# A two-block transformer and state-space kernel: the state-space stage as three interleaved chains, and probabilities transposed through a diagonal tile

## What is computed

```python
# MLA, by query block of 128; DSA has the same softmax over its selected keys
s = jnp.where(key_pos[None, :] <= q_pos[:, None], s, -jnp.inf)
p = jax.nn.softmax(s, axis=-1).astype(v.dtype)
return jnp.einsum('bhqk,bkhv->bqhv', p, v)

# ssd_scan, chunks of 128 tokens, 4 groups of 8 heads of 64 channels, state 128
a_cum = jnp.cumsum(adt, axis=2)
seg = a_cum[:, :, :, None] - a_cum[:, :, None, :]
decay = jnp.exp(jnp.where(tri, seg, -jnp.inf))
cb = jnp.einsum("bclgn,bcsgn->bclsg", cm, bm)
y_diag = jnp.einsum("bclsgr,bcsgrp->bclgrp", cb[..., None] * decay, x)
states = jnp.einsum("bclgn,bclgrp->bcgrpn", bm, x * decay_states[..., None])
...                       # recurrence over the 4 chunks gives prev
y_off = jnp.einsum("bclgn,bcgrpn->bclgrp", cm, prev) * jnp.exp(a_cum)[..., None]
y = y_diag + y_off + d_skip * xh
# gated_group_rmsnorm
u = y * jax.nn.silu(z)
u = u * lax.rsqrt(jnp.mean(u * u over the group) + EPS)
y_ssm = (u * g) @ w_ssm_out
merged = jax.nn.sigmoid(g_att) * y_att + jax.nn.sigmoid(g_ssm) * y_ssm
```

## Time and profile before

| | |
|---|---|
| runs, median (lowest to highest), 3 runs | 2856.41 us (2852.3 to 2861.36) |
| the profiled execution | 2849.98 us |
| its span, first to last instruction | 2848.2 us |
| mean granted TensorE clock | 0.962 |
| PE busy | 2662.3 us, 93%, 11724 instructions |
| PEld busy | 2070.7 us, 73% |
| DVE, ACT, POOL busy | 1448.1 (51%), 663.1 (23%), 1142.3 us (40%) |
| DMA | 436.62 MB, 153 GB/s |

### The profile page before, as it was taken

The page is one execution under the profiler, slowest core; times in us unless marked ns, Lnnn a source line. Parts: engine busy times, 40 slices in busy tenths (PEclk is TensorE's granted clock), DMA queues, the critical chain, the costliest instruction groups (busy, mean ns, idle before and its releaser), DMA issues.

```text
span 2848.2 us, 30951 instructions
## 1 busy us (share of the span) xinstructions
PE 2662.3 (93%) x11724; PEld 2070.7 (73%) x11724; DVE 1448.1 (51%) x1985; ACT 663.1 (23%) x1297; POOL 1142.3 (40%) x764
## 2 busy tenths in 40 slices
PE   8999899999999999999999999999888778899998
PEld 6888688888666578888876777766555546688886
DVE  4754574565544435546566744544334447555521
ACT  2004420111233312102132133322213232222200
POOL 4333355555312145555544533322222113455554
PEclk9999999999899999999999999999888879999999
DMA  6433465656312156565644744434433214465565
GB/s 200 125 115 123 129 192 194 193 194 195 122 60 76 43 167 190 194 195 189 210 156 152 229 148 154 157 126 133 159 123 117 96 45 140 146 195 194 191 195 168
DMA packets 148857, 436.62 MB, mean 153 GB/s; under 512 B 13872, under 2 KB 18160, under 8 KB 148720
## 3 DMA queue, kind: packets, MB, share of 16 engines
q1 hardware_dynamic: 64224, 200.29, 23.9%
q0 software_dynamic: 67584, 201.35, 20.2%
q10 hardware_dynamic: 16912, 33.14, 3.2%
HBM read 417.90 MB, written 16.83 MB: 153 GB/s over the span
## 4 chain that ended last, share of the span: by engine, by line
issue 38%; PE 32%; POOL 23%; DVE 3%; DMA 2%; ACT 2%; DVEq 1%; ACTq 0%; POOLq 0%; SPq 0%
POOL w_lo L450 18%; PE bank L502 9%; PE bank L504 8%; PE bank L505 8%; POOL w_hi L432 5%; PE bank L703 1%; DMA projections<-spill_out 1%; PE bank L1117 1%; PE bank L777 0%; PE bank L780 0%; PE bank L779 0%; DMA residual<-x_in 0%; PE bank L1077 0%; DVE next_gained L2234 0%; PE bank L1107 0%
## 5 line engine op out<-in xcount | busy, mean ns | idle before, releaser
L450 POOL TENSOR_TENSOR w_lo<-w_raw,w_hi 128x1024 fp32r<-128x1024 f32 x376 | 908.9, 2418 | 15.1 <-DMA w_hi<-stream 7.1
L432 POOL DMA_DIRECT2D w_hi<-stream x376 | 227.2, 604 | 1673.1 <-PE bank L502 1505.4
L502 PE MATMUL bank<-x_hi,w_hi 128*128 128x512 f32 x1472 | 590.5, 401 | 26.8 <-POOL w_lo L450 13.5
L504 PE MATMUL bank<-x_lo,w_hi 128*128 128x512 f32 x1472 | 578.6, 393 | 0.0
L505 PE MATMUL bank<-x_hi,w_lo 128*128 128x512 f32 x1472 | 578.0, 393 | 0.0
L502 PEld LDWEIGHTS bank<-x_hi,w_hi 128*128 128x128 f32 x1472 | 279.8, 190 | 96.9 <-issue 20.9
L505 PEld LDWEIGHTS bank<-x_hi,w_lo 128*128 128x128 f32 x1472 | 279.6, 190 | 59.7
L504 PEld LDWEIGHTS bank<-x_lo,w_hi 128*128 128x128 f32 x1472 | 279.9, 190 | 57.5 <-issue 2.4
L1983 DVE TENSOR_TENSOR relu_sq<-relu 128x512 f32<-128x512 f32 x64 | 179.1, 2799 | 94.6 <-ACT relu L1395 94.6
L502 PE MATMUL bank<-hidden_hi,w_hi 128*128 128x512 f32 x512 | 199.2, 389 | 0.0
L504 PE MATMUL bank<-hidden_lo,w_hi 128*128 128x512 f32 x512 | 199.2, 389 | 0.0
(11 more groups left out here) (435 smaller groups left out, 4450.8 us busy)
## 6 DMA issues: line engine op xcount, KB each, us to landing
w_hi<-stream POOLq DMA_DIRECT2D x376, 512.0 KB, 4.8
w_raw<-stream SPq DMA_DIRECT2D x376, 512.0 KB, 3.7
projections<-spill_out ACTq DMA_DIRECT2D x56, 256.0 KB, 2.0
ssm_x<-projections ACTq DMA_DIRECT2D x4, 1024.0 KB, 7.2
gate_tiles<-projections ACTq DMA_DIRECT2D x16, 256.0 KB, 3.2
ssm_z<-projections ACTq DMA_DIRECT2D x4, 1024.0 KB, 9.5
residual<-x_in SPq DMA_DIRECT2D x4, 512.0 KB, 10.7
toeplitz_hi<-toeplitz_rows_hi POOLq DMA_DIRECT2D x4, 512.0 KB, 6.5
```

The costliest lines, as they stand in the source:

```text
L432: e.dma_start(in_slot(whi, t % SLOTS, o), in_stream(o)).then_inc(hi_ready[t % SLOTS], 16)
L450: e.tensor_tensor(wlo[:, s, :], raw[:, s, :], whi[:, s, :].bitcast(F32), ALU.subtract).then_inc(lo_ready, 1)
L502: mm = e.matmul(out, wh, rh, start=first, stop=False)
L504: e.matmul(out, wh, rl, start=False, stop=False)
```

## The change

**Transposes.** In both attentions VectorE no longer scales the row of exponentials. It multiplies the 128x128 identity by the column of inverse sums, and TensorE multiplies each 128x128 tile of exponentials by this diagonal tile, which transposes and scales at once. The call is `matmul` with float32 operands where it was `transpose`.

**State space.** The phases become one sequence of 16 head-pair steps (HEAD_STEPS). Into steps 1, 2 and 3 of a group the preparation of the next group is dealt out (PREP_AT: T0 to T2, then T3, B and S0, then S1 and S2); the one of group 0 stands ahead (PREP). The group before is finished beside it: gating, squares and sums one pair behind (gate_y, square, sum_y), the sum of squares after own_past of step 0, its root on ScalarE in step 1 between the exponentials and past_decay, norm_y at the end of VectorE's step 1, low_y in step 2 ahead of `decayed`. Transposed x, b and states get a second buffer, y a tile of its own (ssm_y), z comes pair by pair in a ring of two, gates in a ring of two. The sum of squares moves from bank 3 to bank 4, so the first transpose of groups 2 and 3 waits for y_rstd. load_x(0) moves into the sparse attention, at item 61.

```diff
@@ attention, TensorE (the same in both)
-                            mm = e.transpose(bank[3 + m % 2][:, chunk(k)], mpr[:, m % 3, chunk(k)], ident)
+                            mm = e.matmul(bank[3 + m % 2][:, chunk(k)], mpr[:, m % 3, chunk(k)], mdiag[:, m % 3, :],
+                                          start=True, stop=True)
@@ attention, VectorE (the same in both)
-                        ts(mpr[:, m % 3, 0:w], mpr[:, m % 3, 0:w], mri[:, m:m + 1], None, ALU.mult).then_inc(at_p, 1)
+                        ts(mdiag[:, m % 3, :], ident, mri[:, m:m + 1], None, ALU.mult).then_inc(at_p, 1)
@@ state space, order of units
+HEAD_STEPS = [(g, p) for g in range(4) for p in range(4)]
+PREP = ["T0", "T1", "T2", "T3", "B", "S0", "S1", "S2"]
+PREP_AT = {1: ["T0", "T1", "T2"], 2: ["T3", "B", "S0"], 3: ["S1", "S2"]}
+        ("first", 0): "a0", ("first", 3): "a1", ("first", 6): "a2",
+        (0, 0, 1): "a3", (0, 1, 1): "a4", (0, 2, 1): "a5", (0, 3, 1): "a6", (1, 0, 1): "a7",
+        (1, 2, 2): "o00", (1, 2, 3): "o01", (1, 3, 1): "o02", (1, 3, 2): "o03 o04", (2, 0, 1): "o05 o06",
+        (2, 0, 2): "o07",
...
+        ("last", 0): "o24 o25", ("last", 1): "o26 o27", ("last", 2): "o30 o31 o32 o33 o34 o35 o36 o37"}.items():
@@ sparse attention, ScalarE
+                    if n == 61:
+                        e.wait_ge(at_s, n0 + 48)
...
+                        load_x(0)
@@ state space, TensorE
+                def squares_sum(g):
+                    e.wait_ge(y_sum, 3 * g + 3)
+                    if g < 3:
+                        e.wait_ge(e_add, 3 * (g + 1) + 3)
+                    else:
+                        e.wait_ge(y_rstd, 3)
+                    e.matmul(bank[4][:, :], ones, ysum[:, :], start=True, stop=True).then_inc(y_full, 1)
+                def prep(g, task):
+                    kind, c = task[0], int(task[1:] or 0)
+                    if kind == "T":
+                        if c:
+                            e.wait_ge(e_tx, 4 * g + c)
+                        else:
+                            e.wait_ge(x_loaded2[g % 2], 48 * (g // 2) + 48)
+                            if g == 1:
+                                e.wait_ge(e_add, 3)
+                            elif g:
+                                e.wait_ge(y_rstd, g - 1)
...
+                for g, p in HEAD_STEPS:
+                    n = 4 * g + p
+                    tasks = (PREP_AT.get(p, []) if g < 3 else []) + [None] * 3
+                    rows(n)
+                    units(g, p, 1)
+                    if tasks[0]:
+                        prep(g + 1, tasks[0])
+                    decay_rows(n)
+                    units(g, p, 2)
+                    if tasks[1]:
+                        prep(g + 1, tasks[1])
+                    own_past(n)
+                    if p == 3 and g < 3:
+                        products(g + 1)
+                    if p == 0 and g:
+                        squares_sum(g - 1)
+                    if tasks[2]:
+                        prep(g + 1, tasks[2])
+                    units(g, p, 3)
@@ state space, ScalarE
+                for g, p in HEAD_STEPS:
+                    n = 4 * g + p
+                    exponentials(n)
+                    if p == 0 and 1 <= g < 3:
+                        e.wait_ge(sg_yd, 4 * g)
+                        load_x(g + 1)
+                    units(g, p, 1)
+                    if p == 1 and g:
+                        root(g - 1)
+                    past_decay(n)
+                    units(g, p, 2)
+                    if n:
+                        square(n - 1)
+                        if n < 15:
+                            load_z(n + 1)
+                    if p == 2 and g < 3:
+                        natural_b(g + 1)
+                    units(g, p, 3)
+                    if p == 1 and g:
+                        his(g - 1)
@@ state space, VectorE
+                for g, p in HEAD_STEPS:
...
+                    if n:
+                        take_y(n - 1)
+                        gate_y(n - 1)
+                    if p == 2 and g:
+                        low_y(g - 1)
+                    decayed(n)
+                    units(g, p, 1)
+                    if tasks[0]:
+                        prep(g + 1, tasks[0])
+                    units(g, p, 2)
+                    if tasks[1]:
+                        prep(g + 1, tasks[1])
+                    if n:
+                        sum_y(n - 1)
+                    if tasks[2]:
+                        prep(g + 1, tasks[2])
+                    units(g, p, 3)
+                    if p == 1 and g:
                         norm_y(g - 1)
```

More of the change, by code:

```diff
@@ L130 @@
 SPILL_SLOTS = 3
+FIRST_GROUP = [SPILL_AT["xb", 0, m] for m in (16, 20, 0, 1, 2, 3)]
 MLP_ORDER = [half_pairs(FIRST[n], 2) + whole_tiles(FIRST[n] + 4, 60) for n in ("mlp0_up0", "mlp1_up0")]
@@ new lines, in products @@
+                def products(g):
+                    for c in range(ST):
+                        mm = e.matmul(bank[5][:, chunk(c)], sb[g % 2][:, chunk(c)], sc[g % 2][:, chunk(c)],
+                                      start=True, stop=True)
+                    mm.then_inc(e_cb, 1)
+                def squares_sum(g):
[5 more added lines that the diff above has]
+                    e.matmul(bank[4][:, :], ones, ysum[:, :], start=True, stop=True).then_inc(y_full, 1)
@@ new lines, in prep @@
+                def prep(g, task):
[9 more added lines that the diff above has]
+                                e.wait_ge(y_rstd, g - 1)
+                        for t in range(4):
+                            mm = e.transpose(bank[4][:, chunk(t)], sx[g % 2][:, t, chunk(c)], ident)
+                        mm.then_inc(e_t, 1)
+                    elif kind == "B":
@@ L1224, in state_space @@
[L1224 to L1232 removed]
+                    else:
+                        e.wait_ge(st_dve, 3 * g + c + 1)
+                        if c:
+                            e.wait_ge(e_add, 3 * g + c)
+                        else:
+                            e.wait_ge(e_bn, g + 1)
+                        e.matmul(bank[4][:, :], sbn[g % 2][:, c, :], sxd[:, :], start=True, stop=True).then_inc(st_pe, 1)
@@ new lines, in state_space @@
+                for i, task in enumerate(PREP):
+                    prep(0, task)
+                    if i == 0:
+                        products(0)
+                    units("first", i)
+                for g, p in HEAD_STEPS:
[17 more added lines that the diff above has]
+                    units(g, p, 3)
@@ L1234, in state_space @@
+                units("last", 0)
+                squares_sum(3)
+                units("last", 1)
+                units("last", 2)
                 f = flow["w_out"]
@@ new lines, in root, with his @@
+                def root(g):
+                    e.wait_ge(y_full, g + 1)
+                    e.activation(grs[:, :], bank[4][:, :], ACT.Ln, scale=0.25 / 512, bias=col("eps"))
+                    e.drain()
+                    e.activation(grs[:, :], grs[:, :], ACT.Exp, scale=-0.5).then_inc(y_rstd, 1)
+                def his(g):
+                    e.wait_ge(un_full, UNIT_AT["o", g - 1, 7] + 1 if g else UNIT_AT["a", 0, 7] + 1)
+                    for k in range(4):
+                        e.wait_ge(y_n, 4 * g + k + 1)
+                        e.activation(yh[:, k, :], yy[g % 2][:, k, :], ACT.Copy).then_inc(y_hi, 1)
@@ new lines, in state_space @@
+                for k in range(2):
+                    load_z(k)
+                for i, task in enumerate(PREP):
+                    if task == "B":
+                        natural_b(0)
+                    units("first", i)
+                for g, p in HEAD_STEPS:
[18 more added lines that the diff above has]
+                        his(g - 1)
@@ L1707, in state_space @@
+                square(15)
+                units("last", 0)
+                root(3)
+                units("last", 1)
+                his(3)
+                units("last", 2)
                 for m in range(8):
@@ L2427, in state_space @@
+                take_y(15)
+                gate_y(15)
+                sum_y(15)
+                units("last", 0)
+                norm_y(3)
+                units("last", 1)
+                low_y(3)
                 for m in range(9):
```

430 lines of the change are left out of this document (155 added, 275 removed), and 9 rows, old and new, of tables (E_STEPS, E_UNITS).

## The result

| | before | after |
|---|---|---|
| runs, median (lowest to highest) | 2856.2 us (2852.3 to 2861.36), 4 runs | 2819.3 us (2815.54 to 2822.97), 4 runs |
| ratio, with its 95% interval | | 0.987 (0.9848 to 0.9891) |
| the profiled execution | 2849.98 us | 2817.55 us |
| its span | 2848.2 us | 2815.7 us |
| mean granted TensorE clock | 0.962 | 0.973 |

The changed kernel is 36.9 us faster by the medians and 32.5 us shorter by the spans. I forecast 17. TensorE has 320 instructions more, is busy 9.4 us longer, and is done sooner.

A forecast was written before the change was run, and what follows sets the result against it. TensorE was taken to bound both attentions and no engine the state-space stage, which could give back gaps and clock. Attentions +27 and stage -44 (317 against 361) sum to -17 us, median 2839; range 2805 to 2872.

The forecast's parts named there:

- Attentions, +27: Both attentions: a second TensorE instruction per tile adds 36 us, smaller gaps return 9; +27, between +13 and +36.
- the price of 106 us: Attentions: addition if true FP32 took four passes; the forecast did not use it, since the trace showed two instructions.
- The state-space stage's sum at full clock, 283: State-space stage: lead-in 28, group 0 51, groups 1 to 3 58, 59 and 49, tail 38; 283 us.
- the tail 4 us of gap: State-space tail: 38 us with one 4 us gap, since root, norm_y and his of group 3 lie behind o24 to o27.
- The longest gaps: State-space stage: longest TensorE gaps of 5 to 7 us in three places, released by y_rstd or the exponential behind it.
- Clock and stalls: State-space stage: 15 us clock cost in groups 1 to 3, 12 in the rest, 6 for stalls, 1 for gate ring.
- the gate ring: State-space tail: two-slot ring issues DMAs two tiles ahead instead of three; a microsecond or two, 1 us in the sum.
- The 6 us of stalls: State-space steps p=1, p=2: stalling VectorE operations lie on the chain of these pairs; 6 us.
- The early load: Sparse attention, item 61: first x, b and c asked for earlier, so the 5.4 us DMA wait goes.
- attention work hidden: Rival, attentions: VectorE sets the pace, so the second pass fills idle time; attentions +5, 2817 us; chance 0.13.
- clock by real matmuls: Rival, attentions: diagonal matmuls count as work for the clock where transposes do not, returning 19 us; 2820 us; chance 0.07.
- Slower by the root chain: Rival, groups 1 to 3: the serial root chain takes 9 us more in each; +13, 2869 us; chance 0.13.

The follow-up runs named there:

- experiment 1: Changed kernel with both attentions put back to scaled rows and identity transposes, state-space stage as changed: 2790.55 us, ratio 0.9783 to the kernel before.
- 9: Kernel before the change with only both attentions' transposes and scalings changed to the diagonal form: 2882.59 us, ratio 1.0108 to the kernel before.
- experiment 7: Changed kernel with root at the end of ScalarE's step p=0 and norm_y ahead of decayed of p=1: 2811.51 us, ratio 0.9847 to the kernel before.
- Experiment 3: Changed kernel with load_x(0) asked for at the start of the state-space stage again: 2829.7 us, ratio 0.9919 to the kernel before.
- experiment 4: Changed kernel with root's logarithm replaced by a copy, so neither table load is needed: 2815.71 us, ratio 0.9865 to the kernel before.
- experiment 6: Changed kernel with both attentions' exponentials and diagonal tiles in float32r, one instruction per tile: 2797.2 us, ratio 0.9794 to the kernel before.
- 8: Changed kernel with root and norm_y moved earlier and both attentions' old transposes back: 2786.7 us, ratio 0.9754 to the kernel before.
- 10: As 8, with decayed ahead of low_y at p=2 and the output unit needing low_y one slot later: 2793.16 us, ratio 0.9783.
- 11: As 10, with low_y further back, behind the last ssm_x_nat and the scaled x: 2786.09 us, ratio 0.9755 to the kernel before.
- 2: Changed kernel with only the first attention put back as before: 2803.2 us, ratio 0.9826 to the kernel before.

## Why the prediction was right or wrong

- **Attentions, +27: right.** Measured +17.0 and +10.2, with +15 and +12 forecast. The pitch read from rows 3 gave 18 us of work for each; the traces show 19.5 and 18.3. What was hidden came out at 2.8 and 7.1 us, where I took 3 and 6. The Trainium skill, Perfetto Trace Analysis, Optimizing Tensor Performance (transpose, not a standard matmul), had spoken against this part, and experiments 1 and 9 agree: without it the change is worth 62 us (experiment 1 against the kernel before on its chip) and not 37. The Trainium skill, FP8 and Floating Point Precision, TensorE Precision Notes, has four passes for true FP32; the price of 106 us worked out from four isn't seen. The page isn't contradicted by that: in the trace of before an f32 product over 512 columns is two instructions of 0.43 us, 0.86 in all, and a float32r product of that width takes 0.23. What was wrong was to take 0.11 us, the pitch of an f32 transpose, for one pass.
- **The state-space stage's sum at full clock, 283: right in sum, in part by luck.** 301.3 less 19.7 of clock is 281.6. By parts, at the clock that was granted: lead-in 30.9 (28 forecast), group 0 50.7 (51), the groups 61.0, 62.9 and 51.1 (58, 59 and 49), tail 44.5 (38). The groups, less their 16.8 of clock, are 8 us shorter than my sum, the tail is 5 us longer and the lead-in 1, and these nearly cancel. I gave the tail 4 us of gap, and TensorE is idle 8.7 us in it. Five VectorE operations there that take 0.56 to 0.74 us alone took 1.5 to 3.4 while POOL's w_lo ran, 10.6 us more in all. The unit behind one of them waited:

```profile
2364.57 3.09 DVE L2467 SCALAR_TENSOR_TENSOR x_lo<-ssm_out_sum,x_hi 128x512 fp32r<-128x512 f32 x1
2364.72 2.39 POOL L456 TENSOR_TENSOR w_lo<-w_raw,w_hi 128x1024 fp32r<-128x1024 f32 x1
2368.32 0.50 PE L508 MATMUL bank<-y_hi,w_hi 128*128 128x512 f32 x1 [2.15 <-DVE ssm_out_sum L2458]
```

- **The longest gaps: right.** Three, of 6.3 us (6.5 forecast), in the places and with the releasers named.
- **Clock and stalls: the step that was mis-sized.** I added 27 us for the clock and 7 for stalls and the gate ring. The clock cost 19.7: 16.8 in groups 1 to 3 (15 forecast) and 2.9 in the rest (12 forecast). Group 0 ran at a clock of 1.00 in after, the tail at 0.97. Before, those parts had lost 17.5 us, and I let most of it stand though I had just removed the gaps that the loss lay behind. The 6 us of stalls aren't on the pairs p=1, p=2, where I put them: low_y took 2.49 us in after, and POOL's w_lo began 0.1 us behind it. They were a real danger there, as experiment 7 shows, where it took 5.24; in after they fell on the tail instead (above). TensorE has no wait for a gate tile, for which I added 1. Together, 34 us against 19.7, that is 14 of the 16 us by which the stage beat the forecast (-60 against -44).
- **The rest of the miss** lies outside the spans. The medians differ by 36.9 us, the spans by 32.5; the profile of before was 6 us under its median, that of after 2.
- **The early load** was costed at the 5.4 us of rows 5. Experiment 3 shows 10 to 16. The stage's sum had it implicitly, since the lead-in was worked out without any wait.
- **Rivals.** By number alone the measured 2819.3 lies under the forecast's 2822 to 2847 and beside two rivals, 2817 (attention work hidden) and 2820 (clock by real matmuls). That is chance: what both name isn't there. *Slower by the root chain*: the gap and the chain exist, but each group is 11 to 18 us shorter than its stretch was before. *Attention work hidden*: excluded by 1 and 9. *Clock by real matmuls*: in the first attention the cost of the clock is 10.2 us after and 10.0 before, in the sparse one 9.1 and 10.1 with the old transposes; nothing of 19 us came back (experiments 4 and 7, with the same attentions as after, have 12.8 in the sparse one, so a microsecond is no sign). The Trainium skill, TensorE: Matmul & The Clock Gate, Part 4, has it that transposes don't count as busy in the same way; no effect of that is seen here.

What stays open: why the profiled execution of experiment 6 lost 15 us more to the clock in the attentions than that of experiment 1, with the same number of TensorE instructions; and how much of the gap between 8 and a stage without half clock could be had, since no run kept the clock up and the chain short at once.

## What to carry to other kernels

Split a stretch into work, idle and clock cost before predicting it, and where an edit removes the gaps, take away the clock's cost behind them too, stretch by stretch. A transpose replaced by an f32 product against a diagonal costs a second instruction on TensorE; here the idle time that it could fill gave back 10 us of the 38. When a long wait is taken out of a chain that runs over three engines, look at what each later operation will then stand beside: a VectorE operation that slid under POOL's took back part of it.

## What the runs showed of the hardware

- The granted clock falls within or right behind TensorE's longer gaps, and the work behind them pays. Two stretches of after, with the clock in the third column from the end: the gap of 6.34 us, and the 6.8 us of work behind it.

```profile
2174.50:2180.80 6.30, 0.03 (x1) 0.00 (x0) 1.29 (x2) 6.06 (x12) 0.00 (x0) 0.62 0.00 0
2180.90:2187.70 6.80, 6.80 (x37) 4.99 (x38) 1.50 (x3) 1.12 (x2) 0.00 (x0) 0.61 0.14 39
```

  A gap of 3.5 us (experiment 4) was followed by the same loss as one of 6.3: 18.6 us in the three groups, against 16.8.
- An elementwise VectorE operation (128x512, f32, SBUF to SBUF) that overlaps POOL's w_lo can take 3.4 us in place of 0.69; this moved from low_y to the scaled x when the order changed (experiments 7, 8, 10, 11). In the thirteen traces, from 2050 us of the span on, 2143 such operations overlap no w_lo, and none of them took over 0.76 us; 578 overlap one, and 509 of these took over 0.8. No run took w_lo away, so the cause is inferred from the coincidence.
- Between executions of the same code the clock's cost of a whole attention differs: 10.1 and 13.6 us in the first (experiments 1 and 2), at the same work of 218.9 and 218.8; 9.1 and 12.8 us in the sparse one (after and experiment 4), at 402.7 and 402.5. That is some 3 us in a span which no edit caused.
